# Delta rule, first stage: VectorE takes the chunks two by two

## What is computed

```
gcum  = cumsum(log_a)                         # per chunk and head
decay = exp(where(i >= j, gcum_i - gcum_j, -inf))
lower = where(i > j, (kb @ k.T) * decay, 0)   # kb = k * beta
t_inv = inverse(eye + lower)
q_att = (q @ k.T) * decay
```

## Time and profile before

| what | value |
|---|---|
| median of 3 runs | 3286.96 us |
| the profiled execution | 3272.47 us, its span 3270.7 us |
| TensorE (PE) busy | 2939.3 us, 90% |
| VectorE (DVE) busy | 1259.3 us, 39% |
| ScalarE (ACT) busy | 901.1 us, 28% |
| GpSimd (POOL) busy | 206.3 us, 6% |
| granted clock of TensorE, mean over the span | 0.94 |
| data moved by DMA | 173.10 MB, mean 53 GB/s |

### The profile page before, as it was taken

How to read it: one execution, slowest core, us unless ns; L and a number is a source line. 1 busy time by engine, 2 the same in 40 slices (tenths; PEclk the granted TensorE clock), 3 DMA queues, 4 the chain that set the end, 5 groups by cost and what they waited for, 6 DMA issues and landing times. The chain is left out here.

```text
span 3270.7 us, 35830 instructions
## 1 busy us (share of the span) xinstructions
PE 2939.3 (90%) x15708; PEld 2291.4 (70%) x15708; DVE 1259.3 (39%) x1855; ACT 901.1 (28%) x1232; POOL 206.3 (6%) x214
## 2 busy tenths in 40 slices
PE   8967879899999897999999896887899888989997
PEld 4646769655786585888888564777755664758886
DVE  2335336100572524333423333625310563353444
ACT  4171111130002535222222417111131114442222
POOL 1001220200000300000000000121200002000000
PEclk9888899899989898999999998888899999999999
DMA  6111040211222000122221010000011001113331
GB/s 206 40 32 60 1 154 1 91 39 52 78 104 70 26 28 25 65 65 65 65 65 65 27 52 26 1 1 1 1 39 52 26 3 42 50 54 98 96 99 56
DMA packets 143362, 173.10 MB, mean 53 GB/s; under 512 B 5398, under 2 KB 116760, under 8 KB 143207
## 3 DMA queue, kind: packets, MB, share of 16 engines
q1 hardware_dynamic: 142256, 170.36, 15.9%
q0 software_dynamic: 672, 0.37, 0.1%
q10 hardware_dynamic: 279, 0.09, 0.0%
HBM read 168.71 MB, written 2.10 MB: 52 GB/s over the span
## 5 line engine op out<-in xcount | busy, mean ns | idle before, releaser
L509 PE MATMUL ps<-modulated,weights 128*128 128x512 f32 (+3 forms) x1920 | 662.2, 508 | 17.8 <-ACT modulated L1042 10.4
L509 PEld LDWEIGHTS ps<-modulated,weights 128*128 128x128 f32 (+1 forms) x1920 | 368.5, 192 | 306.0 <-issue 279.3
L937 PE MATMUL ps<-region_r 128*128 128x512 f32 (+1 forms) x1536 | 376.3, 353 | 0.0
L937 PEld LDWEIGHTS ps<-region_r 128*128 128x128 f32 x1536 | 270.7, 188 | 40.9
L937 PE MATMUL ps<-modulated_r,region_r 128*128 128x512 f32 (+1 forms) x768 | 233.8, 359 | 19.0 <-DVE modulated_r L1670 18.8
L937 PE MATMUL ps<-mixed_r,region_r 128*128 128x512 f32 (+1 forms) x768 | 231.8, 357 | 0.0
L937 PE MATMUL ps<-mixed_r,weights_r 128*128 128x512 f32 (+1 forms) x768 | 231.7, 356 | 0.0
L937 PE MATMUL ps<-region_r,weights_r 128*128 128x512 f32 (+1 forms) x768 | 229.6, 353 | 0.0
L1328 DVE TENSOR_TENSOR weights_r<-weights,region_r 128x2048 fp32r<-128x2048 f32 x64 | 146.4, 2288 | 147.3 <-ACT region_r L1018 147.3
L677 PE MATMUL ps<-region,mixed 128*128 128x128 f32 x1728 | 194.9, 275 | 0.0
L677 PEld LDWEIGHTS ps<-region,mixed 128*128 128x128 f32 x1728 | 193.9, 192 | 0.0
(11 more groups left out here) (278 smaller groups left out, 4003.5 us busy)
## 6 DMA issues: line engine op xcount, KB each, us to landing
weights<-in_w_mlp SPq DMA_DIRECT2D x64, 1024.0 KB, 5.3
weights<-in_w_ada SPq DMA_DIRECT2D x40, 1024.0 KB, 5.2
weights<-in_w_in SPq DMA_DIRECT2D x34, 1024.0 KB, 5.2
region<-in_w_ada SPq DMA_DIRECT2D x8, 1024.0 KB, 17.2
weights<-in_w_out SPq DMA_DIRECT2D x8, 1024.0 KB, 5.1
modulated<-in_x SPq DMA_DIRECT2D x2, 1024.0 KB, 9.9
out<-region SPq DMA_DIRECT2D x4, 512.0 KB, 2.7
weights<-in_w_in SPq DMA_DIRECT2D x2, 640.0 KB, 5.8
```

The source lines that it names most:

```text
L509: last = mm(dst[0:m, CTX + a:CTX + b], w[:, k, m0:m0 + m], rhs[:, k, a:b], start=(first and k == 0), stop=(final and k == ks - 1))
L937: last = mm(dst[:, CTX + a:CTX + b], w[:, k, m], r[:, a:b], start=(k == 0 and r is r_low), stop=(k == KB - 1 and w is low))
```

## The change

Only VectorE's order changes. The new order is e0, e1, m0, m1, e2, e3, m2, m3, e4, e5, m4, m5. No instruction, wait or buffer is added or removed; the streams of the other engines are the same.

```diff
-                    for ci in range(NC):
+                    for ci in range(0, NC, 2):
                         exponents(ci)
-                        if ci:
-                            matrices(ci - 1)
-                    matrices(NC - 1)
+                        exponents(ci + 1)
+                        matrices(ci)
+                        matrices(ci + 1)
```

## The result

| | before | after |
|---|---|---|
| first comparison, median | 3286.22 us (4 runs, 3283.18 to 3290.99) | 3232.21 us (4 runs, 3226.73 to 3236.81) |
| ratio, with its 95% interval | | 0.9847 [0.9815, 0.9878] |
| a second comparison, more runs | 3277.2 us (29 runs, 3257.65 to 3291.67) | 3236.77 us (6 runs, 3225.51 to 3239.99) |
| ratio, with its 95% interval | | 0.9893 [0.9867, 0.9918] |
| the profiled execution | 3272.47 us, span 3270.7 | 3236.81 us, span 3235.0 |

The kernel is faster. The medians lie 54 us apart in the first comparison and 40 us in the second; by the ratio, which is not simply that of the medians, it is 50 us (40 to 61 by the interval) and 35 us (27 to 44).

A forecast was written before the change was run, and what follows sets the result against it. The stage was taken as one chain, TensorE, `exponents`, `matrices`, TensorE. Terms 22.6 + 2.0 + 9.2 = 33.8 us, taken from the median of 3286.96 us, gave 3253 us, range 3240 to 3267 us.

The forecast's parts named there:

- Parts 1 and 2: Four stage passes: one VectorE leg less in each pair, 22.58 us, and no ramp between a pair's chunks, 2.0 us.
- Part 3: TensorE's bursts in the four passes: the lower clock costs 20.4 us before, 11.2 us after, giving back 9.2 us.
- Parts at nothing: Bank reads beside TensorE's writes, GpSimd's masks and layer 0's ring of weight loads: each expected to cost nothing.
- The sum against the profile: Whole kernel: 33.8 us less than the profiled execution of 3272.47 us, giving 3238.7 us.
- The step that failed: Whole kernel: the same 33.8 us taken from the shown median, 3286.96 us, giving the forecast of 3253 us.
- B: TensorE's clock stays high in the paired bursts; sum 45 us, 3242 us; chance 14%.
- A: TensorE's clock gives nothing back in the longer bursts; 22 to 27 us less, some 3262 us; chance 18%.
- C: TensorE stops between a pair's chunks all the same; 0 to 6 us less, 3281 to 3287 us; chance 4%.
- D: Later work: TensorE's lower clock costs more there, making the kernel slower, 3302 us at 25% more; chance 3%.
- A sign that I sized wrongly: Per pass, two VectorE waits for L653 over 3 us, those of chunks 3 and 5 about 1.5 us at full clock.

The follow-up runs named there:

- e0: Not a run: VectorE's `exponents` for chunk 0 of a pass, first in VectorE's order; no time of its own as a run.
- e5: Not a run: VectorE's `exponents` for chunk 5 of a pass, the last chunk; no time of its own as a run.
- the products: 8 more TensorE products before each wait for `p1_done`: old order 3250.86 us, 0.9921; new order, before even chunks only, 3218.50 us, 0.9829; against 3279.89 us.
- the new order with 10 products a pass: The new order with 10 more TensorE products ahead of chunk 1 of each pass: 3233.69 us, 0.9899 against before.
- after, again: The kernel after, unchanged, in a new execution: 3236.77 us (6 runs), 0.9893 against before; its four passes took 130.0 us.
- each_early: VectorE does `exponents` then `matrices` chunk by chunk; ScalarE copies even points' rows earlier; against before: 3220.23 us, 0.9832, then 3211.16 us, 0.9829.

## Why the prediction was wrong, step by step

- **Parts 1 and 2, the leg and the ramp, 24.6 us.** Right: 24.6 us once the clock is taken out of both orders, and right in each layer: 12.7 us in layer 0, as forecast (11.88 + 0.8), and 11.9 in layer 1 (10.70 + 1.24).
- **Part 3, the clock.** Right in kind, somewhat off in size. I took 8 x 1.4 = 11.2 us for the new order; it was 9.5 us. Six of the 8 pairs paid, 1.5 to 1.6 us each; the first pair of each pass of layer 1 paid nothing in the profiles of the new kernel. I had given all 8 a gap of 3.0 to 3.3 us, though the earlier trace rows show 1.82 us ahead of that first pair. The short gap is no rule either: in the old order, layer 1 backward, the burst after 1.81 us was slow, and VectorE waited 4.57 us for it:

```profile
2221.78 1.16 PE L649 MATMUL ps<-k_f_sb,gdn_small 128*128 128x128 f32 x8 [1.81 <-DVE region L1464]
...
2224.34 1.91 PE L653 MATMUL ps<-region 128*128 128x128 f32 x8
```

- **The clock in the old order.** I miscounted the bursts: 12 paid, one of them 2.9 us, and four paid nothing, three of layer 0 and one of layer 1; the sums don't hang on it. That the clock costs the old order 20.4 us was true of the one profile. Over the profiles above the old passes take 170 us, and over those that stand for the new order 131 us.
- **The Trainium skill's rule** (TensorE: Matmul & The Clock Gate, section "HAM oscillation — how this bites in real kernels"), that a burst after a long enough wait starts throttled, fits the new order better than I had allowed: all six pairs after 3.0 to 3.3 us of idle were slow, and none was once products filled the gap. It still doesn't fit every burst of the old order: the one at 456.64 ran at full clock after 3.32 us, and the same one in the second profile at half.
- **Parts at nothing.** All held: L1464 beside TensorE's writes to the other banks took 341 to 346 ns (339 to 346 before), no wait within a pair, none for a load, none for a mask.
- **The sum against the profile.** 3238.7 us forecast; the two profiled executions of the new order took 3236.81 and 3234.68 us. The passes and some luck make this agreement, since the differences in the rest of the span cancelled.
- **The step that failed** is the one from there to the median: "The median shown is 14.5 us above the profiled time; from it, 3286.96 - 33.8", and the "some 4 us for the phases of the later work and the spread of the median". The three runs shown lay within 8 us of each other, and I took their median as the kernel's. In 77 runs, over all comparisons, the old order takes 3255.7 to 3291.67 us, median 3274.4, and the profile's 3272.47 us lies in the middle of them. The new order takes 3225.51 to 3239.99 us in 10 runs, median 3235.8: 38.6 us less, which agrees with the 39 us of the mean passes. So my starting point was 12.6 us too high and the range far too narrow for it. The spread was in sight: the profile 11 us below the lowest of three runs. (By its own terms the range should also have begun at 3238 us, B's 3242 less 4.)
- **What this leaves open** is why the first comparison found 54 us where the passes give 36 to 39. All four of its runs of before lie at 3283.18 us or above, as only 9 of the other 73 do; drawn by chance from the same executions, that would be rare (an estimate: (9/73)^4, one in some 4000). Something that held for the old order in that comparison alone isn't excluded, and no run here tells.
- **Why the old order scatters more** may lie in a consequence that I hadn't drawn: 16 gaps, each of which may or may not cost 1.4 to 2.9 us by where it falls, against 8. Shown are the 8.3 us in one pass of one program. Against its being the larger part of the 36 us stands the rest of the span, outside the four passes: it goes from 3089.9 to 3116.9 us over the 14 profiles, 27 us.
- **Rivals.** A and B fall by the products, C by the timeline. D asked whether the work outside the passes moves: the last section shows that it does, by 8.9 us against the change in one stretch and 7.2 us for it in another. The first doesn't go with the order; whether the second does isn't settled.
- **A sign that I sized wrongly**: VectorE's waits for L653 in a pass of layer 0 are all over 3 us (4.30 and 3.37), since the odd chunk there has the columns and the point before it, and only layer 1's second waits are near the 1.5 us I gave (1.39 and 1.60 forward). The passes got shorter by 9.4, 6.5, 8.9 and 10.6 us, where I had given 9 and 8.

## What to carry to other kernels

With two sets of buffers between two engines, look at what stands in the consumer's queue before the release of the set that the producer needs next: an evacuation of new data ahead of the release of old data turns two sets into one, whatever the busy shares say. In this kernel short TensorE bursts with gaps of 1.8 to 3.3 us between them cost the clock on top, and both longer bursts (20.4 down to 9.5 us) and products without use in the gap won part or nearly all of it back. And before a forecast is set on a median of three, compare it with the profiled execution: if they differ by more than the three do, the distance between them is the least width of what isn't known.

## What the runs showed of the hardware that I hadn't expected

The MLP of layer 0 has two levels that don't go with the order. From its first to its last product that reads `region_r` alone (L937) it takes 465.3 to 465.4 us in seven of the 14 profiles and 474.3 us in the other seven, old order and new among both. A stretch at either level, from two kernels of the new order (columns: busy us and count of PE, PEld, DVE, ACT and POOL, granted clock, DMA share, GB/s):

```profile
1600.00:1620.00 20.00, 20.00 (x118) 17.62 (x117) 7.99 (x6) 3.99 (x4) 0.00 (x0) 1.00 0.28 94
```

```profile
1600.00:1620.00 20.00, 20.00 (x115) 17.33 (x115) 5.94 (x5) 3.52 (x3) 0.00 (x0) 1.00 0.16 53
```

(the first is of the new order with 10 products a pass, the second of after, again). The granted clock is 1.00 in both, and TensorE does 118 or 115 records in 20 us, for the whole of the stretch. In the first pair of profiles before had the fast level and after the slow one, 8.9 us against the change, made up for by other stretches of layer 0, the HGRN2 recurrence most: from its first L806 to its last it took 87.5 us before and 80.3 after. This one isn't free of doubt as to the order. The long value stands in four profiles, three of the six with the old order in layer 0 and one of the two of `each_early`'s order, and in none of the five with the new order by pairs.

The MLP's level may be a part of the spread of the runs. The 10 runs of the new order fall in two groups, 3 at 3225.5 to 3228.0 us and 7 at 3234.7 to 3240.0, and both profiled ones are in the upper group and have the slow level. The other runs have no profile, so this isn't shown. What sets the level stays open; no run here was made on it.
